# A decoder trunk with routed experts: the first five expert weight slots are loaded ahead of the last six conditioning rows

## The reference

```python
for l in range(DEPTH):                       # DEPTH = 2
    mod = (c_act @ w_mod[l] + b_mod[l])[:, None, :]
    sh1, sc1, g1, sh2, sc2, g2 = jnp.split(mod, 6, axis=-1)
    h = x * (1.0 + sc1) + sh1
    y = hybrid_mixer(h, w_in[l], w_a2[l], b_a[l], gla_norm_g[l], w_out[l])
    x = layer_norm(DN_ALPHA * x + (1.0 + g1) * y, ln_g[l, 0], ln_b[l, 0])
    h = x * (1.0 + sc2) + sh2
    if l % 2 == 0:
        y = swiglu(h, ffn_w_gate[j], ffn_w_up[j], ffn_w_down[j])
    else:
        y = moe_swiglu(h, w_router[j], b_router[j], moe_w_gate[j], moe_w_up[j], moe_w_down[j])
    x = layer_norm(DN_ALPHA * x + (1.0 + g2) * y, ln_g[l, 1], ln_b[l, 1])
```

## Time and profile before

| | us |
|---|---|
| median of 3 runs | 1241.91 (1241.63 to 1243.26) |
| profiled execution, its own time | 1238.05 |
| its span | 1236.3 |
| PE busy | 1146.2 (93%) |
| DVE busy | 548.2 (44%) |
| first expert product starts at | 523.85 |

### The profile page before, as it was taken

The page is one execution under the profiler, slowest core; times in us unless marked ns, Lnnn a source line. Parts: engine busy times, 40 slices in busy tenths (PEclk is TensorE's granted clock), DMA queues, the critical chain, the costliest instruction groups (busy, mean ns, idle before and its releaser), DMA issues.

```text
span 1236.3 us, 25859 instructions
## 1 busy us (share of the span) xinstructions
PE 1146.2 (93%) x11020; PEld 625.6 (51%) x11020; DVE 548.2 (44%) x886; ACT 281.9 (23%) x482; POOL 67.1 (5%) x118
## 2 busy tenths in 40 slices
PE   1899879999998899799999999999999999999985
PEld 1789867778878898523333333333333333233322
DVE  6799888687757999740121121011201211210225
ACT  0556334334426664310010010000100100100100
POOL 2100000000112001010000000000000000000101
PEclk9999989999999999899999999999999999999998
DMA  9974777999965846999999999999999999999991
GB/s 337 311 259 137 277 251 290 340 359 392 359 204 161 283 151 213 403 408 385 411 399 411 411 398 413 412 396 412 410 391 412 404 399 408 395 402 411 412 397 65
DMA packets 156952, 423.08 MB, mean 342 GB/s; under 512 B 21052, under 2 KB 75104, under 8 KB 145568
## 3 DMA queue, kind: packets, MB, share of 16 engines
q1 hardware_dynamic: 146720, 395.16, 83.8%
q0 software_dynamic: 6080, 20.31, 4.5%
q10 hardware_dynamic: 4032, 5.90, 1.4%
HBM read 405.60 MB, written 15.73 MB: 341 GB/s over the span
## 4 chain that ended last, share of the span: by engine, by line
PE 54%; SPq 11%; DVE 6%; DMA 5%; issue 2%; ACT 1%; POOL 0%; DVEq 0%; ACTq 0%
PE bank L1363 27%; PE bank L1377 15%; SPq L487 4%; SPq L488 4%; PE bank L341 4%; PE bank L343 3%; PE bank L342 3%; DMA raw_w<-in_moe_w_down_dram 3%; SPq L497 2%; DVE u_low L1538 1%; DMA u_raw<-in_w_in_dram 1%; DMA raw_u<-in_ffn_w_up_dram 1%; DVE mod_acc L1527 1%; DVE score L1582 0%; PE bank L964 0%
## 5 line engine op out<-in xcount | busy, mean ns | idle before, releaser
L1363 PE MATMUL bank<-raw_w,xg 128*32 128x512 f32 (+1 forms) x4608 | 461.3, 559 | 7.3 <-DMA raw_w<-in_moe_w_up_dram 4.6
L1363 PEld LDWEIGHTS bank<-raw_w,xg 128*32 128x32 f32 x4608 | 154.3, 110 | 311.4 <-issue 303.3
L1914 DVE TENSOR_TENSOR he<-he,bank 128x256 f32<-128x256 f32 (+1 forms) x72 | 25.7, 384 | 527.4 <-ACT he L895 527.2
L1377 PE MATMUL bank<-raw_w,heT 128*32 128x512 f32 x2112 | 231.2, 592 | 2.7 <-DMA raw_w<-in_moe_w_down_dram 2.7
L895 ACT ACTIVATE he<-bank 128x256 f32<-128x256 f32 (+1 forms) x72 | 21.2, 367 | 577.9 <-PE bank L1363 577.9
L1377 PEld LDWEIGHTS bank<-raw_w,heT 128*32 128x32 f32 x2112 | 71.3, 110 | 156.2 <-issue 153.6
L1527 DVE SCALAR_TENSOR_TENSOR mod_acc<-mod_row,c_act,mod_acc 128x1024 f32<-128x1024 f32 x70 | 89.9, 1284 | 6.8 <-DVE mod_acc L1527 0.9
L341 PE MATMUL bank<-u_high,hT_H 128*128 128x256 f32 x256 | 75.2, 294 | 3.4 <-DVE u_low L1538 2.6
L343 PE MATMUL bank<-u_high,hT_L 128*128 128x256 f32 x256 | 72.4, 283 | 0.0
L342 PE MATMUL bank<-u_low,hT_H 128*128 128x256 f32 x256 | 72.4, 283 | 0.0
L341 PE MATMUL bank<-gu_H,hT_H 128*128 128x512 f32 x160 | 64.8, 405 | 0.0
(11 more groups left out here) (299 smaller groups left out, 1251.7 us busy)
## 6 DMA issues: line engine op xcount, KB each, us to landing
raw_w<-in_moe_w_down_dram SPq DMA_DIRECT2D x88, 1024.0 KB, 17.1
raw_w<-in_moe_w_gate_dram SPq DMA_DIRECT2D x128, 512.0 KB, 13.3
raw_w<-in_moe_w_up_dram SPq DMA_DIRECT2D x128, 512.0 KB, 15.5
mod_row<-in_w_mod_dram SPq DMA_DIRECT2D x80, 512.0 KB, 6.8
raw_w<-in_moe_w_gate_dram SPq DMA_DIRECT2D x64, 384.0 KB, 11.8
raw_w<-in_moe_w_up_dram SPq DMA_DIRECT2D x64, 384.0 KB, 13.8
u_raw<-in_w_in_dram SPq DMA_DIRECT2D x20, 1024.0 KB, 7.3
raw_d<-in_ffn_w_down_dram SPq DMA_DIRECT2D x11, 1024.0 KB, 10.8
```

What stands on the lines that cost most here:

```text
L1363: last = mm(bank[g][32 * q:32 * q + 32, 0:2 * HALF[c]].rearrange("s (m j r) -> s m j r", m=2, r=64), xg[:, i, g, k, :], cols[:, :, :, 64 * ...
L1377: last = mm(bank[3 + g][32 * q:32 * q + 32, :], heT[(par + c) % 2][:, g, 2 * a + b, :], W[:, b, h * 512:(h + 1) * 512], start=(c == 0 and ...
L1914: V.tensor_tensor(h, h, bank[g][:, w:2 * w].rearrange("s (j c b) -> s j b c", b=2, c=32), ALU.mult).then_inc(s["m_hid"], 1)
```

## The change

In SP's list the first eight weight slots are cut in two. Five of them (`EARLY = 5`, ten transfers) now stand between rows 73 and 74. They wait for `pv_ps` at 4 and `ycat` at 3 (the gates multiplied into the mixer's output, L1724). Behind them come rows 74 to 79, then the wait for `yT_L` at 8 and the other three slots. No instruction of another engine is touched, and the number of transfers and of bytes is the same.

```diff
+EARLY = 5
@@
-            load_mod_rows(*range(74, len(MOD_ROWS)))
-
             mg, mu, md = moe_w_gate[0], moe_w_up[0], moe_w_down[0]
-            sp.wait_ge(s["yT_L"], 8)
@@
-            def load_gate_up(e, pr, n, c):
+            def load_gate_up(e, pr, n, c, tiles=range(KT)):
 
                 f = slice(CHUNK_AT[c], CHUNK_AT[c] + CHUNK_W[c])
-                for k in range(KT):
+                for k in tiles:
                     i = (FIRST + n + k) % NRAW
@@
-            load_gate_up(0, 0, -FIRST, 0)
+            sp.wait_ge(s["pv_ps"], 4)
+            sp.wait_ge(s["ycat"], 3)
+            load_gate_up(0, 0, -FIRST, 0, range(EARLY))
+            load_mod_rows(*range(74, len(MOD_ROWS)))
+            sp.wait_ge(s["yT_L"], 8)
+            load_gate_up(0, 0, -FIRST, 0, range(EARLY, KT))
             sp.wait_ge(s["proj"], 2 * NU)
```

## The result

| | before | changed |
|---|---|---|
| median of 7 runs each, us | 1243.19 | 1247.95 |
| lowest and highest | 1240.43, 1244.57 | 1245.63, 1249.97 |
| profiled span | 1236.3 | 1246.7 |
| first expert product at | 523.85 | 534.31 |
| from there to the end of the span | 712.5 | 712.4 |

The changed kernel is slower: ratio 1.0042, 95% interval 1.003 to 1.0055, which is 5.2 us (3.7 to 6.8). The last two rows of the table hold most of the explanation: the first expert product comes later, and from there on nothing has changed.

What follows compares the result with a forecast made beforehand. In the experts' part products and transfers run at almost one pace, and transfers decide the end. Late rows 5.4 + clock 0.8 - gain 0 = 6.2 us, so 1241.9 + 6.2 = 1248.1, range 1244.0 to 1251.5.

Steps and rivals of the forecast that it cites:

- Part one: SP's early weight issues: ten from 472.8 to 479.4, row 74 issued at 479.4, 0.5 us later on SP.
- Part two: Landing of rows 74 and 75 behind ten weight transfers: row 75 at 493.9, the middle of 492.4 and 495.3.
- The 358 GB/s of the Trainium skill: HBM limit per core: five slots would take 14.6 us, fast end 1.8 us later; the sum left it out.
- Part three: DVE at row 75: starts 5.4 us late, bounds 3.9 and 8.1; PE's gap grows from 0.6 to 6.0 us.
- Part four: PE's clock behind its gap before `u_low`: a half-speed stretch costing 0.8 us, with 0 and 1.7 as ends.
- Part five: Experts' part: earlier weights gain 0, the lead is used up, and PE's 7.3 us of weight waits stay.
- the dip at 568: DMA rate falls from 567 to 570 us; the queue runs dry there, using up any lead at the latest.
- The sum: Whole kernel: 5.4 + 0.8 - 0 = 6.2 us slower, median 1248.1.
- The rows are not late: Rows 74 and 75 share the DMA engines and arrive by 488; time 1242 to 1243; chance 0.10.
- The lead is kept: Experts' part: PE's weight waits fall by 5 us; chance 0.03 for under 1239.4, 0.02 more for about 1243.
- the third: Rival at PE's gap: slow end for row 75 and a longer clock stretch; 1251 to 1254; chance 0.10.

Runs made afterwards that it cites:

- filled: Changed kernel plus 60 products into an unread bank on PE where it waits for `u_low`; 1.004 (1.0022 to 1.0058) of the kernel before.
- early2: Changed kernel with two early weight slots instead of five; 0.9996 (0.998 to 1.0012) of the kernel before.
- early3: Changed kernel with three early weight slots instead of five; 1.0011 (0.9996 to 1.0026) of the kernel before.
- pool_rows: Changed kernel with rows 74 to 77 loaded by POOL in its own queue; 1.002 (1.0009 to 1.0031) of the kernel before, 2.5 us slower.
- rows_first: Changed kernel with rows 74 to 77 issued ahead of the early weights, and four early slots; 1.001 (0.9992 to 1.0028) of the kernel before.
- down_order: Kernel before with the first expert's down slots asked for in order 0, 1, 2, 3, each once free; ratio 1.0004 (0.9989 to 1.0018).
- rows_first_down: Changed kernel, rows 74 to 77 ahead of four early slots, first expert's down slots in order 0, 1, 2, 3; 0.9997 of the kernel before.

## Why the prediction held, and where it was off

**Part one** held but for a detail. The ten weight issues ran from 474.20 to 479.89, 5.7 us and not 6.6, and were done before `yT_L` came; row 74 was issued with it, at 480.96. SP lost nothing.

**Part two** took row 75 to land 21.1 us behind the first weight issue (493.9 - 472.8). It was 22.0 (496.2 - 474.2), inside the bounds. The choice between them had a wrong reason. The burst was hardly slow: the DMA engines moved 353 GB/s up to 480, and 411 and 412 GB/s from 480 to 498, with nothing of POOL's load among it before row 74 was in. What took the time was that the last of the 16 parts of a transfer comes late: by the landings in the trace row 74's first part is in at 491.2 and its last at 494.6. The full rate alone would have had it, behind row 73's landing at 478.3, at 478.3 + 12.8 + 1.3 = 492.4. My middle between full rate and measured pace came out about right because the measured pace may have had this in it; that was luck more than reasoning.

**The 358 GB/s of the Trainium skill** ("DMA: Bandwidth & Descriptors", Specifications), which the prediction set beside the rows, are not what this core had: 412 GB/s from 486 to 498.

**Part three**: 5.4 us expected, 5.85 measured as wait, 5.6 in the distance from row 72's to row 79's addition (18.4 against 12.8 us). Rows 76 to 79 cost nothing more, as said. PE's gap grew to 7.1 us, not 6.0; kernels with their rows in time have gaps of 0.7 to 1.6 us there.

**Part four** had the right mechanism and counted too little. The half-speed stretch came, and longer than I had taken (6.8 us and not 3.5; PE worked in 4.0 of it). DVE then waited 1.62 us for PE's last product, where it had not waited before: twice the 0.8 us that I counted, and near my upper end of 1.7. In `filled`, without the stretch, the wait was 0.29 us. The times of the runs can't confirm so small a term.

**Part five** held: 7 traces (before, changed, early2, early3, pool_rows, filled, rows_first) have 712.4 to 713.1 us from the first product to the end, with leads from none to five slots. The two with the other order of the first down slots have 714.2 (`down_order`, with its extra half clock) and 710.4 (`rows_first_down`). I had named the dip at 568 as the place where a lead is lost at the latest. It is only the last of three: the changed kernel had already stood still from 506.5 to 514 and from 531.5 to 538. Of the 2.2 MB of lead 0.2 MB were left 10 us behind the first product, long before the dip, so the full ring ahead of the first freed buffers is where it is lost. That fits `rows_first_down`, which had the dip closed and was no faster by a measurable amount.

**The sum** was 6.2 us, with 5.4 for the rows; the runs have 5.2 (3.7 to 6.8). That it came so near is in part luck. The two terms as the traces have them, 5.6 and 1.6, make 7.2 us, a little more than the interval allows, and what takes the difference away between the medians is not shown.

**The rivals.** "The rows are not late" fell with DVE's wait. "The lead is kept" fell with `rows_first`. Of the third, the longer clock stretch was there, with 1.6 us, but not the late end for row 75, and the time did not reach its 1251 us.

## What to carry to other kernels

Before a load is moved ahead, ask two things of the trace: how many bytes the idle DMA time at the new place holds, since whatever is more than that delays what stands behind it in the queue; and whether the loads further on are still timed by the consumer, through a ring of buffers. Where they are, and the ring is full before the consumer starts, a lead ends there, and only a lag would be felt: measure both sides, since a kernel can stand just at the bend. If a few small loads that a busy engine needs are due at the same time, put them ahead of the bulk rather than in a second queue: here that left 0.5 us of waits for rows (`rows_first`, four early slots) against 3.6 us (`pool_rows`, five). Count also the engine behind the one that waits: its clock can fall in the gap, and the first engine then waits for it.

## What the runs showed of the hardware that I had not expected

- Two queues with work shared the DMA engines about evenly, though SP's backlog was the larger: in `pool_rows` POOL's rows of 0.52 MB came 2.56 us apart beside it, where the whole rate of 411 GB/s would make it 1.3, and from 484 to 486 us the two queues moved 0.39 and 0.41 MB.
- A transfer's 16 parts don't end together: row 74 of the changed kernel had 3.4 us between its first and its last part, and came 2.2 us behind what the bytes alone give. Rows 74 to 77 had 0.6 to 1.9 us in the kernel before. It isn't the same each time: in `filled`, behind the same ten transfers, row 74 had 1.9 us.
- 48 more matmuls on PE ahead of a loop came with pauses of 4.6 and 4.8 us at two turns of the loop, in which PE waited for nothing that the profile shows. It is one trace; no other kernel here, `filled` with its 60 more matmuls included, had more than 0.6 us of such time in the experts' part. The cause wasn't sought.
